# Attention outputs scaled once a head pair in place of normalised probabilities, in a hybrid decoder step on one core

## The reference, cut to what matters

```python
u = rmsnorm(x); p = u @ w_in            # q, k, v | z | x, B, C | dt
# group A: attention of every head under three dilated windows, merged by their denominators
# group B: causal convolution on x, B, C, then a chunked scan, gate, norm
h = x + concat(A, B) @ w_out
y = h + relu(rmsnorm(h) @ w_up)**2 @ w_down
```

## Time and profile before

| | us |
|---|---|
| median of three runs | 1978.06 |
| the three runs | 1971.88, 1978.06, 1979.29 |
| the profiled execution | 1971.67 |
| its span in the profile | 1969.7 |

### The profile page before, as it was taken

One profiled execution on the slowest core, in us unless ns is written; L12 is line 12 of the kernel. 1 busy time (PEld: TensorE's weight loads), 2 busy tenths in 40 slices (PEclk: granted clock), 3 DMA queues, 4 the chain that ended last, 5 costly groups with the idle time before them and its releaser, 6 DMA issues.

```text
span 1969.7 us, 33409 instructions
## 1 busy us (share of the span) xinstructions
PE 1861.3 (94%) x12776; PEld 1705.5 (87%) x12776; DVE 1414.6 (72%) x1897; ACT 892.5 (45%) x1610; POOL 1103.7 (56%) x846
## 2 busy tenths in 40 slices
PE   8999999989888999989997999989999999999999
PEld 7999999878777888855556789989999998999999
DVE  5888721777766666559987755788776778878777
ACT  5344413566665677546654002234333344444442
POOL 4688630866757666524443223334555557878775
PEclk9999999999999999979997999989999999999999
DMA  4354434443452434389995444213334348444442
GB/s 179 140 186 166 177 129 125 95 108 97 103 129 63 125 114 123 95 265 326 317 314 199 174 171 179 76 65 149 153 120 162 139 179 314 154 153 142 139 139 96
DMA packets 139097, 309.31 MB, mean 157 GB/s; under 512 B 31659, under 2 KB 65323, under 8 KB 135228
## 3 DMA queue, kind: packets, MB, share of 16 engines
q1 hardware_dynamic: 114924, 270.60, 40.8%
q10 hardware_dynamic: 24016, 36.58, 5.5%
HBM read 222.42 MB, written 93.28 MB: 160 GB/s over the span
## 4 chain that ended last, share of the span: by engine, by line
PE 55%; DVE 13%; issue 6%; ACT 6%; POOL 1%; DMA 1%; ACTq 0%; DVEq 0%; SPq 0%; POOLq 0%
PE ff_ps L2585 30%; PE dense_ps L973 7%; PE wo_psa L2422 5%; PE wo_psb L2554 2%; DVE att_p L1078 2%; PE att_t_ps L1002 2%; ACT att_p L1172 1%; PE wo_psa L2554 1%; PE att_s_ps L991 1%; PE ssd_in L1638 1%; ACT att_qhi L1189 1%; PE sa_s L1551 1%; DVE ssd_m L1879 1%; PE sa_s L1555 1%; PE att_s_ps L992 1%
## 5 line engine op out<-in xcount | busy, mean ns | idle before, releaser
L2585 PE MATMUL ff_ps<-ff_set,ff_wring 128*128 128x264 f32 x5376 | 662.1, 286 | 12.4 <-DVE ff_set L3070 4.5
L2585 PEld LDWEIGHTS ff_ps<-ff_set,ff_wring 128*128 128x128 f32 x5376 | 659.3, 189 | 14.8 <-DVE ff_set L3070 4.7
L920 POOL TENSOR_SCALAR att_p<-att_p,att_rden 128x128 f32<-128x128 f32 (+7 forms) x128 | 250.6, 1965 | 135.9 <-DVE att_rden L1060 135.8
L2256 POOL TENSOR_TENSOR ff_wring<-const,ff_wring 128x256 fp32r<-128x256 f32 (+1 forms) x192 | 211.5, 1106 | 148.6 <-ACT ff_wring L2750 148.5
L2750 ACT ACTIVATE ff_wring<-const 128x256 fp32r<-128x256 f32 (+1 forms) x192 | 93.5, 489 | 225.5 <-PE ff_ps L2585 114.2
L1065 DVE TENSOR_TENSOR att_pTlo<-att_t_ps,att_pThi 128x512 fp32r<-128x512 f32 x192 | 106.1, 553 | 117.0 <-ACT att_pThi L1180 115.4
L3219 DVE TENSOR_TENSOR h<-h,ff_ps 128x528 f32<-128x528 f32 x192 | 133.0, 699 | 49.2 <-PE ff_ps L2585 46.4
L1180 ACT ACTIVATE att_pThi<-att_t_ps 128x512 fp32r<-128x512 f32 x192 | 93.2, 487 | 130.4 <-PE att_t_ps L1002 120.9
L973 PE MATMUL dense_ps<-u_hi,w_hi 128*128 128x352 f32 x480 | 116.9, 346 | 16.2 <-DVE conv_pre L1092 7.8
L2256 POOL TENSOR_TENSOR ff_wring<-wo_raw,ff_wring 128x256 fp32r<-128x256 f32 (+1 forms) x72 | 84.4, 1172 | 63.4 <-ACT ff_wring L2750 63.4
L680 DVE RECIPROCAL proj_rinv<-proj_rinv 128x1056 f32<-128x1056 f32 x16 | 108.1, 6753 | 9.7 <-ACT proj_rinv L570 9.7
(11 more groups left out here) (366 smaller groups left out, 4339.4 us busy)
## 6 DMA issues: line engine op xcount, KB each, us to landing
tmp_r_sets<-h SPq DMA_DIRECT2D x16, 1848.0 KB, 5.9
ff_setraw<-tmp_r_sets SPq DMA_DIRECT2D x56, 528.0 KB, 5.7
sa_k<-in_cache_k SPq DMA_DIRECT2D x32, 640.0 KB, 9.0
sa_v<-in_cache_v SPq DMA_DIRECT2D x40, 512.0 KB, 4.8
w_raw<-in_w_feat SPq DMA_DIRECT2D x36, 512.0 KB, 6.3
out_qk<-proj_out SPq DMA_DIRECT2D x16, 528.0 KB, 8.0
tmp_bias_rows<-tmp_table ACTq DMA_DIRECT2D x8, 1024.0 KB
att_bias<-tmp_bias_rows SPq DMA_DIRECT2D x16, 512.0 KB, 3.5
```

Of the source, the lines that this page charges most:

```text
L920: pool.tensor_scalar(slot(h, qt), slot(h, qt), rden[:, qt, :], None, ALU.mult).then_inc(normed, 1)
L2256: pool.tensor_tensor(w_set(n)[:, 1], operand(q, m), w_set(n)[:, 0].bitcast(F32), ALU.subtract).then_inc(fw_split, 1)
L2585: mm = pe.matmul(ff_ps[:, (b + g) * 512:(b + g) * 512 + HG], ws[:, wi, k, :], xs[:, xi, k, g * HG:(g + 1) * HG], start=(opens and k == 0 a ...
```

## The change

The probabilities stay as ScalarE's exponential leaves them. `invert` makes the reciprocals of all eight tiles of a head at once. A pair of heads' reciprocals are stored to DRAM in the order of tokens (`tmp_rden`) and read back as two rows, each broadcast over the 64 partitions of a head, into the second slot of the ring's `w_raw`; from the third woven weight tile on, all weights go through the first slot. Once a pair's outputs are added, GpSimd multiplies the 128x1024 of `att_oT` by these rows (`scale_out`), and both stores of the pair wait for that.

```diff
+    def place(self, n):
+
+        return n % 2 if n < ONE_RAW else 0
+
     def load(self, eng, dram, n):
 
         if n >= 2:
-            eng.wait_ge(self.split, max(2 * (n - 1), 3))
-        eng.dma_start(self.raw[:, n % 2, :], dram["w_feat"][n]).then_inc(self.loaded[n % 2], 16)
+            eng.wait_ge(self.split, 2 * n if n > ONE_RAW else max(2 * (n - 1), 3))
+        eng.dma_start(self.raw[:, self.place(n), :], dram["w_feat"][n]).then_inc(self.loaded[n % 2], 16)
...
+    pair_ends = {n: h // 2 for n, (h, g) in ends.items() if h % 2 and g}
+    inverts = {TICKS * h + 2: h for h in range(NH)}
...
-        busy[n] += 0.16 * (n - 1 in score) + 0.69 * (n in ends) + 0.7 * (n % TICKS == 9)
+        busy[n] += 0.69 * (n in ends) + 0.7 * (n % TICKS == 9)
...
+            def store_inverse(f):
+                sp.wait_ge(inverted, 2 * f + 2)
+                sp.dma_start(dram["rden"][2 * f:2 * f + 2, :].rearrange("h (t p) -> p h t", p=P), rden[:],
+                             allow_slow_non_contiguous=True).then_inc(rden_stored, 16)
+
+            def load_inverse(f):
+                sp.wait_ge(rden_stored, 16 * (f + 1))
+                if f >= 1:
+                    sp.wait_ge(o_scaled, f)
+                else:
+                    sp.wait_ge(ring.split, 2 * ONE_RAW)
+                for j in range(2):
+                    sp.dma_start(rows_inv[j * HD:(j + 1) * HD, :],
+                                 dram["rden"][2 * f + j].partition_broadcast(HD)).then_inc(rows_loaded, 16)
...
+                if n in inverts and inverts[n] % 2:
+                    store_inverse(inverts[n] // 2)
+                if n - 4 in inverts and inverts[n - 4] % 2:
+                    load_inverse(inverts[n - 4] // 2)
...
-            def normalise(h, qt):
-                pool.wait_ge(inverted, rank(h, qt) + 1)
-                pool.tensor_scalar(slot(h, qt), slot(h, qt), rden[:, qt, :], None, ALU.mult).then_inc(normed, 1)
+            def scale_out(f):
+                pool.wait_ge(rows_loaded, 32 * (f + 1))
+                pool.wait_ge(o_kept, 4 * f + 4)
+                pool.tensor_tensor(oT[:], oT[:], rows_inv, ALU.mult).then_inc(o_scaled, 1)
...
-                for h, qt in score.get(n - 1, ()):
-                    normalise(h, qt)
...
+                if n in pair_ends:
+                    scale_out(pair_ends[n])
...
-                pe.wait_ge(normed, NT * h + HALF * (g + 1))
+                pe.wait_ge(exped, NT * h + HALF * (g + 1))
...
-                if h >= 2 and g == 0:
-                    dve.wait_ge(mix_stored[h % 2], 16 * (h // 2))
+                if h >= 2 and h % 2 == 0 and g == 0:
+                    dve.wait_ge(mix_stored[0], 16 * (h // 2))
+                    dve.wait_ge(mix_stored[1], 16 * (h // 2))
...
-            def invert(tiles):
-
-                (h, first), n = tiles[0], len(tiles)
-                dve.wait_ge(exped, rank(h, first) + n)
-                dve.reciprocal(rden[:, first:first + n, 0], den[:, first:first + n, 0]).then_inc(inverted, n)
+            def invert(h):
+                dve.wait_ge(exped, NT * (h + 1))
+                if h >= 2 and h % 2 == 0:
+                    dve.wait_ge(rden_stored, 16 * (h // 2))
+                dve.reciprocal(rden[:, h % 2, :], den[:, :, 0]).then_inc(inverted, 1)
...
-                if n - 1 in score:
-                    invert(score[n - 1])
+                if n in inverts:
+                    invert(inverts[n])
...
+                if h >= 1 and RANK[qt] == 0:
+                    act.wait_ge(inverted, h)
...
-            def store_out(h):
-                act.wait_ge(o_kept, 2 * h + 2)
-                act.dma_start(dram["mix"][h * HD:(h + 1) * HD, :], oT[h % 2 * HD:(h % 2 + 1) * HD, :]
-                              ).then_inc(mix_stored[h % 2], 16)
+            def store_out(f):
+                act.wait_ge(o_scaled, f + 1)
+                for j in range(2):
+                    h = 2 * f + j
+                    act.dma_start(dram["mix"][h * HD:(h + 1) * HD, :], oT[j * HD:(j + 1) * HD, :]).then_inc(mix_stored[j], 16)
...
-                if n - 1 in ends and ends[n - 1][1] == 1:
-                    store_out(ends[n - 1][0])
+                if n - 1 in pair_ends:
+                    store_out(pair_ends[n - 1])
...
+                elif g == 0:
+                    dve.wait_ge(woven.o_scaled, NPAIR)
```

More of the change, by code:

```diff
@@ L42 @@
 QK_TILES, XBC_TILES, Z_TILES = 2 * KD, XBC // P, KD
+ONE_RAW = QK_TILES + 2
 START = 1
@@ L1291 @@
     mix_stored: object
+    o_scaled: object
     tail_stored: object
```

16 lines of the change are left out of this document (9 added, 7 removed).

## The result

| | median, us | range | executions |
|---|---|---|---|
| before | 1974.16 | 1968.33 to 1979.29 | 20 |
| after | 1979.11 | 1971.92 to 1992.84 | 20 |

The ratio is 1.0034, 95% interval 1.0021 to 1.0047: some 7 us slower, where 5 us faster was forecast. The profiled execution of after took 1987.42 us (span 1985.2), 8.3 us above the median of its own runs, and that of before 1971.67, 2.5 us under its median, so some 11 of the 15.5 us between the two spans belong to these two executions. The profile is read for where things happen; how much is read from the ratios.

What follows compares the result with a forecast made beforehand. In the woven stage GpSimd's time was taken as no bound, VectorE as nearer to one. Terms -15 - 2 + 6 + 6 = -5 us gave 1973 us at the median; range 1950 to 1993, forecast case 1965 to 1981.

Steps and rivals of the forecast that it cites:

- Relief: Woven stage: removed GpSimd multiplications, VectorE reciprocals and their waits gain 15 us with convolution, 2 us (0 to 6) without.
- contention: Stretch with convolution: GpSimd instructions slow VectorE's convolution steps and additions; removing them frees a net 3 us of VectorE.
- ScalarE behind `o_scaled`: Pair ends: ScalarE's store waits for the multiplication, delaying keep_high and TensorE's scores; near 1 us a pair, 6 us (0 to 22).
- Two ticks of room: Pair ends: argument against ScalarE being held at every pair, two ticks remain until TensorE needs the piece.
- the prediction's own sign of being wrong: Pair ends: the forecast is wrong if TensorE's waits behind a pair exceed 2 us.
- Rival 2: Pair ends: ScalarE is held at every pair, 22 us lost, 6 at the end, 17 gained; +11, 1989 us; chance 0.15.
- turning point of 2.3 us a pair: Pair ends: the slower rival, ScalarE held, decides once more than 2.3 us a pair reach TensorE.
- Small pieces: Inverses' DMAs: 4-byte stores take 7.2 to 14.4 us, loads 8, covered by 32 us before the multiplication; cost nothing.
- rival 4: Pair ends: inverses' rows come late, 4-byte store over 23 us; 5 us late seven times is 35, 2008 us; chance 0.05.
- End of the stage: Last multiplication delays GpSimd's `sa_qdiag` work: TensorE idles 5.6 us, 2.4 are slack, clock comes on top; 6 us (3 to 8).
- VectorE beside the multiplication: Woven stage: the skill's rule could hold VectorE 2.45 us eight times, 20 us; the sum used the rows' excess, 8.
- The slot and the planner: Woven stage: weight loads waiting for the earlier tile's split are hidden, four convolution steps move by a tick; nothing.

Runs made afterwards that it cites:

- relief_only: Changed kernel without the multiplication of oT, the store and loads of the inverses; mix stores wait for additions only, outputs unnormalised: 1955.22 us, 0.9907 of before.
- best1: sp_but_last with the inverses turned on VectorE, so that they leave as 64 pieces of 128 bytes a pair: 1955.83 us, 0.9909 of before.
- sp_but_last: Changed kernel with SyncE issuing the mix stores of the first seven pairs and ScalarE only the last: 1963.57 us, 0.9947 of before.
- no_rows: Changed kernel without the store and loads of the inverses; the multiplication and ScalarE's wait stay, outputs not divided by the denominators: 1974.22 us, 0.9998 of before.
- wait_kept: best1 with ScalarE again waiting for the multiplication at every pair, but issuing nothing there: 1959.79 us, 0.9922 of before.

## Why the prediction was wrong

The time, 1979.11 us, lies in the range and within the 0.5% called the same, but the forecast was on the wrong side: it had -5 us, and it is +7. Following the versions from the kernel before to the changed one, the ratios give: relief -18.4 (relief_only), multiplication, turned inverses and end, less what SyncE's stores save, +0.4 (best1 minus relief_only), 4-byte pieces +7.5 (sp_but_last minus best1), stores on ScalarE for seven pairs +17.2 (after minus sp_but_last). Each difference is uncertain by 3 to 5 us. Two terms were too small, by 11 and by 7.5 us, and either alone turns the sign; that the time still fell near the forecast is partly luck, since the +6 for the end came back as +0.4 in this sum.

**Relief, -17 forecast: right in size.** Relief_only measured -18.4 us, in both stretches: no step from pair end to pair end of 64 to 68 us is left, and the last step fell from 51.1 to 49.8. By engine GpSimd's share came out as 5 us. The forecast gave contention 3 of VectorE's 28.6 us, which at its rate of 15 us for these is 1.6 us of time, so this part was larger than forecast.

**ScalarE behind `o_scaled`, +6 forecast (0 to 22): the term that failed.** The place and the chain from `keep_high` to TensorE's scores were named, and the term's bounds held it; the size was wrong by some 11 us. The forecast took near 1 us a pair. no_rows against relief_only shows 2.1 us a pair right behind the pair ends and 18.0 in all, after against sp_but_last 17.2. The steps that failed: `keep_high` came 2.7 us late at the seventh pair and not 2.2. "Two ticks of room" was read off one pair early in the stage, where TensorE came to its scores 1.8 us after the minimum's end (554.93, against 552.81 + 0.28); at the seventh pair's end in best1 it came 0.3 us after (779.16, against 778.60 + 0.28), so lateness there goes nearly straight through. TensorE's idleness of 2.23 us, the prediction's own sign of being wrong (over 2 us behind a pair), brought the half clock as the earlier trace rows had shown it, and that was counted at the end of the stage and not here. And the wait of the next addition for both stores had no term, though the diff shows it; it was small, 1.5 us in after. Rival 2 had the right place and nearly the size, 22 us. Of its mechanism, ScalarE held, the bare hold is worth 2.5 us in wait_kept, not clear of noise; it takes the stores behind it to make 17. Its turning point of 2.3 us a pair doesn't follow from its own terms: 17 gained and 6 lost at the end leave 11 us, 1.6 a pair.

**Small pieces, 0 forecast: wrong.** From the store's issue to the loads behind it, it took what the row of 16-byte pieces gave, 10.3 to 13.1 us in its bounds of 7.2 to 14.4, and the rows came in time: rival 4 didn't happen. What failed is "cost nothing": only its own lateness was asked for, not what 2048 pieces do to other transfers. The Trainium skill, DMA: Bandwidth & Descriptors, Rules for kernel authors, advises to rearrange such a last dimension so that it is contiguous; the runs agree, with 7.5 us.

**End of the stage, +6 forecast: size nearly right, cause half right.** From the last addition to the output projection it was 4.8 us longer after (217.8 against 213.0), 2.2 to 2.9 us longer in no_rows and best1 than in relief_only. TensorE idled 5.97 us (5.6 forecast), its scores took 7.51 us in place of 4.74. But ScalarE, held at the last store, was 3.3 us late by itself, and the slack was counted for TensorE alone.

**VectorE beside the multiplication.** A convolution step still took up to 2.457 us (2.392 before). The last `gate`, three equal instructions beside the last multiplication (856.02 to 858.62 us), shows the exclusion better (ns, min/median/max):

```profile
L1155 DVE SCALAR_TENSOR_TENSOR silu_half<-silu_tanh,silu_half x3: 512/526/2659, 855.9 to 858.9; 128x352 f32<-128x352 f32 x3
```

The second of the three, begun at 856.34 us and ended at 859.00, took 2.1 us more than the others, nearly all that was left of the multiplication's 2.60, where the prediction's rows gave 1.0. With the rule of the Trainium skill, SBUF — State Buffer, Who interferes with whom, that the later of the two blocks for the whole instruction of the other, this trace agrees. It cost little: best1 with the same eight multiplications is within 0.6 us of relief_only, though SyncE's stores may hide part of it.

**The slot and the planner: nothing** was forecast, and no run isolates them. TensorE waited for no split. GpSimd waited 92.2 us for weights, 34.0 in relief_only with the same slot, so most of that comes with the small pieces.

## What to carry to other kernels

When a store is made to wait for one more engine, price the whole queue behind it: the wait, the issues that now come late with it, the clock behind TensorE's idleness, and who needs the buffer back and when; then ask which queue has nothing due at that tick, and check that it isn't the one with the next stage's loads. An unchanged total with less work on two engines is no proof that the relief was worthless: take the additions away, all together and then one by one. A transfer in tiny pieces has a price even where nobody waits for it: here the weight loads landed later and VectorE waited longer for another queue's stores.

## What was not expected of the hardware

- 2048 pieces of 4 bytes a pair cost some 7 us in all, and twice as many 36 more, five times as much. The 512 KB weight loads landed in 6.0 us without them and in 7.5 to 8.1 with them. Stores of 16 pieces of 128 bytes land in 1.4 us.
- Leaving one 2.2 us gap in TensorE's work brought the 1.2 GHz level for about 2 us (three dense matmuls 1.08 us, then 0.73); a gap of 1.0 us at the same place did not. A gap of about 2 us doesn't always do it: in wait_kept TensorE was idle for 2.04 us up to 623.54 us, and the granted clock from 621 to 628 us was 1.00.
- With the same program, 20 executions of the changed kernel lay 21 us apart (1971.92 to 1992.84), 20 of the kernel before 11 us, six of best1 7 us (1953.28 to 1960.68). The profiled executions show 23, 20 and 11 windows of 5 us under 0.97 of the clock between 325 and 875 us. That the gaps make the spread was not tested, and by before's 20 windows they don't by themselves.
